# A two-block fp32 layer kernel: tile 0's chain to its first expert picks moved ahead of tile 1's last attention steps

## The reference

```python
cols_lat, cols_ctx = h_lat @ w_in, h_ctx @ w_in          # 256 latent, 256 context tokens
mla_lat = mla_mixer(...)      # 4 heads; latent queries, 512 keys; softmax(q k^T) v
ml_lat  = mlstm_mixer(...)    # 4 heads, two directions, gated linear attention, head norm
x  = x + gt1 * (concat([mla_lat, ml_lat]) @ w_out)
h2 = rmsnorm(x, g_norm2) * (1.0 + sc2) + sh2
x  = x + gt2 * peer(h2, ...)

def peer(xb):                                             # per tile of 128 tokens
    q = (xb @ w_pq).reshape(128, 8, 2, 128)
    s = einsum('thpd,hpkd->thpk', q, sub_keys)            # 8 heads x 2 x 128 keys
    sv, si = top_k(s, 16)                                 # then the 16 best of the 16 x 16 sums
    ...                                                   # -> eidx: 8 x 16 experts per token
    act = gelu(einsum('thkd,td->thk', expert_u[eidx], xb))
    return einsum('thk,thkd->td', g * act, expert_v[eidx])
```

## Time and profile before

| | |
|---|---|
| median of 3 runs | 1698.18 us (1697.4 to 1699.87) |
| profiled execution, first to last instruction | 1697.5 us; no other time of that execution is given |
| mean granted TensorE clock | 0.943 |
| TensorE matmul busy | 1465.2 us (86%) |
| VectorE busy | 1274.4 us (75%) |
| ScalarE busy | 554.8 us (33%) |
| GpSimd busy | 604.5 us (36%) |
| read from HBM | 436.23 MB, 258 GB/s over the span |

### The profile page before, as it was taken

How to read it: one execution, slowest core, us unless ns; L and a number is a source line. 1 busy time by engine, 2 the same in 40 slices (tenths; PEclk the granted TensorE clock), 3 DMA queues, 4 the chain that set the end, 5 groups by cost and what they waited for, 6 DMA issues and landing times.

```text
span 1697.5 us, 22640 instructions
## 1 busy us (share of the span) xinstructions
PE 1465.2 (86%) x7548; PEld 942.4 (56%) x7548; DVE 1274.4 (75%) x2708; ACT 554.8 (33%) x1549; POOL 604.5 (36%) x611
## 2 busy tenths in 40 slices
PE   7998999896969577646648999999999999999997
PEld 2645574343435122212213797699944797699953
DVE  1687777777777777778877687489986688479985
ACT  2234334443434243323322264222201254322210
POOL 0004036777777777777774002100011002100010
PEclk9999999998989799868768999999999999999999
DMA  9885059999999999999999541275553432085141
GB/s 365 304 289 219 24 218 405 409 409 409 409 403 407 409 403 409 390 398 405 398 405 384 193 147 51 77 259 174 175 181 105 149 116 85 28 296 161 51 156 67
DMA packets 170745, 438.77 MB, mean 258 GB/s; under 512 B 12531, under 2 KB 59027, under 8 KB 170500
## 3 DMA queue, kind: packets, MB, share of 16 engines
q0 software_dynamic: 81824, 299.86, 45.1%
q1 hardware_dynamic: 88806, 137.46, 23.3%
HBM read 436.23 MB, written 1.05 MB: 258 GB/s over the span
## 4 chain that ended last, share of the span: by engine, by line
PE 58%; DMA 12%; POOL 10%; DVE 9%; issue 6%; ACT 2%; DVEq 2%; SPq 1%; ACTq 0%; POOLq 0%
PE psum L908 19%; DMA arena<-in_expert_u,indices 11%; PE psum L1313 7%; POOL arena L1497 5%; POOL arena L1490 4%; PE psum L895 3%; PE psum L914 3%; PE psum L896 3%; PE psum L939 2%; DVE arena L2532 2%; PE psum L701 2%; PE psum L1279 2%; PE psum L584 2%; PE psum L1243 2%; PE psum L681 1%
## 5 line engine op out<-in xcount | busy, mean ns | idle before, releaser
L2532 DVE CUSTOM_DVE_ANT_0 arena<-arena,psum 128x1024 f32<-128x1024 f32 x256 | 312.6, 1221 | 142.5 <-DMA arena<-in_expert_u,indices 121.9
L895 PE MATMUL psum<-arena 128*128 128x512 f32 x380 | 237.9, 712 | 184.7 <-ACT arena L1809 182.9
L1490 POOL DMA_INDIRECT arena<-in_expert_u,indices x256 | 259.6, 1014 | 93.4 <-issue 66.3
L1497 POOL DMA_INDIRECT arena<-in_expert_v,indices x255 | 246.9, 968 | 82.6 <-issue 68.6
L895 PEld LDWEIGHTS psum<-arena 128*128 128x128 f32 x380 | 68.0, 213 | 310.0 <-ACT arena L1809 289.0
L896 PE MATMUL psum<-arena 128*128 128x512 f32 x380 | 221.4, 668 | 0.0
L1432 POOL TENSOR_TENSOR small<-small 128x1 f32<-128x1 f32 (+5 forms) x30 | 32.1, 1070 | 485.4 <-DVE small L2738 191.8
L908 PE MATMUL psum<-activations_T,weight_ring 128*128 128x128 f32 x1664 | 194.5, 275 | 0.0
L908 PEld LDWEIGHTS psum<-activations_T,weight_ring 128*128 128x128 f32 x1664 | 190.3, 192 | 1.0 <-issue 0.8
L1797 ACT ACTIVATE activations_T<-activations_T 128x1 f32<-128x1 f32 x256 | 51.9, 203 | 392.9 <-DVE activations_T L2532 392.7
L896 PEld LDWEIGHTS psum<-arena 128*128 128x128 f32 x380 | 82.0, 216 | 109.7 <-issue 109.7
(11 more groups left out here) (499 smaller groups left out, 2478.3 us busy)
## 6 DMA issues: line engine op xcount, KB each, us to landing
weight_ring<-in_ffn_w_in SPq DMA_DIRECT2D x44, 1024.0 KB, 7.7
weight_ring<-in_w_in SPq DMA_DIRECT2D x14, 2048.0 KB, 9.2
weight_ring<-in_w_ada SPq DMA_DIRECT2D x8, 2048.0 KB, 11.2
arena<-in_ffn_w_out POOLq DMA_DIRECT2D x14, 1024.0 KB, 7.0
weight_ring<-in_w_out SPq DMA_DIRECT2D x6, 2048.0 KB, 8.5
weight_ring<-in_w_ada SPq DMA_DIRECT2D x16, 512.0 KB, 9.9
weight_ring<-in_w_pq SPq DMA_DIRECT2D x4, 2048.0 KB, 12.8
weight_ring<-in_ffn_w_out POOLq DMA_DIRECT2D x8, 1024.0 KB, 5.3
```

The source lines that it names most:

```text
L895: mm(o0, DIAG[:, j % ND, :], v_row(n)[:, 0:512], start=m == 0, stop=last)
L1490: nc.gpsimd.indirect_dma_start(u_row(g), None, a["expert_u"], bass.IndirectOffsetOnAxis(ap=where, axis=0)).then_inc(sem(f"u_row{g % NU}"), 16)
L1497: nc.gpsimd.indirect_dma_start(v_row(g), None, a["expert_v"], bass.IndirectOffsetOnAxis(ap=where, axis=0)).then_inc(sem(f"v_row{g % NV}"), 16)
L2532: ttr(out=u_row(n), in0=u_row(n), in1=h2, scale=1.0, scalar=0.0, op0=ALU.mult, op1=ALU.add, accum_out=DOT[:, i, m:m + 1]).then_inc(sem("u_ ...
```

## The change

The first two batches stay, but there DVE takes a step's maximum ahead of the modulation sums (L2075) and copies the step's values after them. From the third batch on the order is new on PE, DVE and ACT. On PE the seventh step (u = 6) comes after tile 0's output product and not before it; the eighth to tenth (u = 7, 8, 9) come in one row after the first scores of both heads. The low half of tile 1's output product, which used to run while DVE searched, comes after them. On ACT batch 3's exponentials stand behind the copy of the first scores, and batch 2's turned weights and value products come after those. On DVE batch 3's product and combination come behind the whole search, with the last maximum ahead and the last three value copies behind. The first scores go to `SC00` in another tile, since `SC` lies where the values `VM` of the late steps still are. POOL gets two waits: g = 0 waits for the last step's scores, g = 2 also for the last step's values.

```diff
+        SC00 = v(3584, 4, NKEYS, of=XT)
 @block.tensor
+            score_products(*BATCHES[2])
+            outputs = [bank_d(), bank_d()]
+            output(outputs[0], 0, 0, 0, 4)
+            output(outputs[1], 0, 1, 0, 1)
+            gated(0, o)
+            output(outputs[1], 0, 1, 1, 4)
+            for b in range(2):
+                output(outputs[b], 0, b, 4, KT).then_inc(d_full, 1)
+            mla()
+            spread(BATCHES[3][1])
             h2_turned(0)
-            mla()
             first_queries(0)
-            mla()
-            heads_taken = c["d"]
-            first_scores(0)
             score_products(*BATCHES[3])
+            first_scores(0)
+            weights_turned(2)
+            value_products(2, BATCHES[2][1])
+            first_queries(1)
+            first_scores(1)
+            for _ in range(3):
+                mla()
+            at["mla_last"] = heads_taken = c["d"]
             outputs = [bank_d() for b in range(2)]
+            h2_back(0, bank_d, sem("h2_back"))
             pe.wait_ge(d_free, heads_taken)
             output(outputs[0], 1, 0, 0, 4)
             output(outputs[1], 1, 1, 0, 4).then_inc(sem("wout_low"), 1)
-            value_products(2, BATCHES[2][1])
-            first_queries(1)
-            first_scores(1)
-            h2_back(0, bank_d, sem("h2_back"))
             weights_turned(3)
             value_products(3, BATCHES[3][1])
 @block.gpsimd
+                if g == 0:
+                    pool.wait_ge(a_full, at["mla_s"][7])
                 if g == 2:
                     pool.wait_ge(sem("ml_p"), 2 * len(BATCHES))
+                    pool.wait_ge(d_full, at["mla_last"])
 @block.scalar
+            exponentials(2)
+            gated(0)
...
+            mla()
             h2_turned(0)
-            mla()
-            exponentials(3)
-            mla()
             first_queries(0)
             first_scores(0)
+            exponentials(3)
+            weights_turned()
             heads_mixed(*BATCHES[2])
             first_queries(1)
             first_scores(1)
+            mla()
             pick_exp(0)
+            mla()
 @block.vector
+            for n in range(2):
+                mla_probabilities()
+                decayed_maxima(n)
+                mla()
+                mla_probabilities()
+                mixed(n)
+                combined()
+                mla_maximum()
+                modulation(10 + n, 11 + n)
...
+                mla_taken()
...
+            mla()
+            h2_end(0)
+            mla_probabilities()
+            decayed_maxima(3)
+            all_of(search(0))
+            mla_maximum()
+            mixed(3)
+            mla_probabilities()
+            dve.wait_ge(a_full, at["comb", 2])
+            combined()
+            for _ in range(3):
+                mla_taken()
```

More of the change, by code:

```diff
@@ L784, in _ @@
             spread(0)
-            for n, (i, hp) in enumerate(BATCHES[:3]):
+            for n, (i, hp) in enumerate(BATCHES[:2]):
                 mla()
                 score_products(i, hp)
[L788 to L793, removed]
-                    mla()
[L795 to L806, removed]
-                    mla()
+                modulation_sum(10 + n)
+                if n == 1:
+                    pe.wait_ge(sem("pool_sum"), 1)
+                    o = bank_d()
+                    mm(o, ONE, MACP, start=True, stop=True).then_inc(d_full, 1)
+                mla()
@@ L808, in _ @@
                 weights_turned(n)
                 spread(BATCHES[n + 1][1])
-                if n < 2:
-                    value_products(n, hp)
+                value_products(n, hp)
+            score_products(*BATCHES[2])
+            wout += [weights()[:, 0:4 * D].rearrange("p (k n) -> p k n", k=4) for half in range(2)]
+            outputs = [bank_d(), bank_d()]
+            output(outputs[0], 0, 0, 0, 4)
+            output(outputs[1], 0, 1, 0, 1)
+            o = bank_a()
+            at["gated"] = c["a"]
@@ L1705, in first_scores @@
                 o = full()
-                act.copy(SC[:, 0, 2 * hh:2 * hh + 2, :], o[:, 0:2 * P].rearrange("p (c k) -> p c k", c=2)).then_inc(a_free, 1)
+                act.copy(SC00[:, 2 * hh:2 * hh + 2, :], o[:, 0:2 * P].rearrange("p (c k) -> p c k", c=2)).then_inc(a_free, 1)
             def pick_exp(k):
@@ L1728, in weights_turned @@
                     act.copy(MLPT[:, hh, :, :], o.rearrange("p (s q) -> p s q", s=4)).then_inc(a_free, 1)
-            for n, (i, hp) in enumerate(BATCHES[:3]):
+            for n, (i, hp) in enumerate(BATCHES[:2]):
                 exponentials(n)
                 mla()
[L1733 to L1739, removed]
                 mla()
                 weights_turned()
-                if n < 2:
-                    heads_mixed(i, hp)
+                heads_mixed(i, hp)
+            exponentials(2)
+            gated(0)
+            for h in range(2):
+                act.wait_ge(sem("x_ready" if h else "x_half"), 1)
+                e = slice(h * 512, h * 512 + 512)
+                ins = af(XSQ[0][:, e], X[:, 0, e], ACT.Square, accum_out=SS[:, 16 + h:17 + h])
+            ins.then_inc(sem("ss_ready"), 1)
+            mla()
             h2_turned(0)
-            mla()
-            exponentials(3)
-            mla()
             first_queries(0)
             first_scores(0)
+            exponentials(3)
+            weights_turned()
             heads_mixed(*BATCHES[2])
@@ L2471, in _ @@
-                if n < 3:
-                    mla()
+                mla_taken()
+            dve.drain()
+            decayed_maxima(2)
+            mla_probabilities()
+            mean_of([(0, 4, VD)])
+            gate(0)
+            mixed(2)
+            combined()
+            dve.wait_ge(sem("g2_in"), 16)
+            stt(MODB[:, 2, :], MODB[:, 2, :], 1.0, G2[:, :], ALU.add, ALU.mult)
+            dve.drain()
+            for b in range(2):
+                e = slice(b * 512, (b + 1) * 512)
+                o = full()
+                tt(MTMP[:, b, :], o, MODB[:, 0, e], ALU.mult).then_inc(d_free, 1)
+                dve.drain()
+                tt(X[:, 0, e], X[:, 0, e], MTMP[:, b, :], ALU.add).then_inc(sem("x_ready" if b else "x_half"), 1)
+                dve.drain()
+                tt(H2[0][:, e], X[:, 0, e], MODB[:, 2, e], ALU.mult)
```

55 lines of the change are left out of this document (21 added, 34 removed).

## The result

The changed kernel takes 1706.67 us (median of 5 runs, 1705.10 to 1708.22) against 1698.18 us for the kernel before: ratio 1.0047, 95% interval 1.0036 to 1.0057. It is 8.5 us slower; 7.8 were forecast. The profiled execution spans 1706.2 us (8.7 more than before) at a mean granted clock of 0.938 (0.943 before); its time, 1708.22 us, is the highest of the five. The totals say little: VectorE's group of dot products has the same busy time, and idles 1.3 us more than in the earlier trace rows.

The account below looks back on a forecast made before the run. DMA engines were taken to bound the picks, the end moving with when gathers run without a stop. Queue loss 7.2 less backlog 1.3 is 5.9, plus clock 1.9 is 7.8: 1698.18 to 1706.0 us, range 1700.5 to 1710 (own range 1702.6 to 1709).

Parts of the forecast that it names:

- First part: Up to the first scores: VectorE's new order and later MLA steps bring them at 215.9, 5.7 us earlier.
- Rival D: Gated heads come later than 193.8 by a us or more, delaying first scores: 1707 to 1708; chance 0.05.
- Second part: From first scores to TensorE's sums: work becomes a chain with two waits, V gather 8 at 268.2, 7.2 us later.
- would show it: List of expected profile signs, such as first gather at 229 to 231, pick 2 near 238, V gather 8 near 268 to 270.
- Clock: TensorE's half clock behind the two new waits: 1.9 us taken, from 0 to 3.8.
- 0 for the second: Clock price of TensorE's second wait taken as 0, since its followers wait for VectorE anyway up to the low outputs.
- Rival C: Both waits drop TensorE's clock for longer, low outputs at half speed: +9.7, 1707.9, up to 1710; chance 0.2.
- I take 1.3: Smaller DMA backlog at V gather 8, by 0.55 MB, gives back 1.3 us of the 7.2; ends 0 and 1.3.
- the 1.5 of the joints: Uncertainty of +-1.5 us for some twelve chain joints read from rows with neighbours of another kind.
- Small edits: `SC00` copy, POOL's wait for the last values, w_pq's later third slice and the earlier `keys` load: 0 each.
- A: Faster: DMA traffic bounds and its first gather starts 3.5 us earlier, so 1694.7; chance 0.07.
- B: No change: exponentials in other work's shadow, TensorE's waits about one us each, about 1699.5; chance 0.15.

Follow-up runs that it names:

- short fill: Changed kernel with 12 idle 128x128 matmuls on TensorE in each of the two 3.1 us waits: 1703.91 us, ratio 1.0033.
- pick 3 early: Changed kernel with tile 1's two low output products moved behind batch 3's turned weights and value products on TensorE: 1705.37 us, ratio 1.0041.
- without the load: Changed kernel with w_pq's third slice not loaded but for a corner, gathers as many: 1707.14 us, ratio 1.0058.
- early VectorE edit: Kernel before; in batches 0 and 1 VectorE takes the next MLA maximum ahead of the modulation sums, the values' copy behind: 1696.75 us, ratio 0.9988.
- both waits shorter: Changed kernel; ScalarE copies batch 2's turned weights before batch 3's exponentials, VectorE takes last probabilities before batch 3's mixing, value copies before its combination: 1700.89 us.

## Why the prediction was right

The forecast of 1706.0 us is 0.7 off the median and inside its range, and most of its steps stand: the loss was made where it said, by the waits and the order that it named. Two terms were mis-sized, and in part it was lucky.

**First part.** Value products of batch 1 at 186.4 (measured 186.39), output product 189.35 (189.33), MLA step 203.6 (203.60), turned h2 208.8 (208.79), first scores 215.9 (215.84). The steps are right; that the dates agree to a tenth is luck, since the other profiles with this order have the first scores anywhere from 213.53 to 215.59. Counted from the 24 small matmuls ahead of the change, they come after 72.34 to 73.43 us in the seven profiles with the new order and after 78.18 to 78.72 in the four with the old one, 5.3 us sooner on average, where 5.7 were forecast. Rival D is out.

**Second part.** With its 1.9 for the first clock drop added to each date from the value products on, the chain said pick 0 231.9 (232.18), h2 turned back 240.0 (239.80), low outputs 240.9 (241.44), pick 3 248.9 (249.62), last value products 249.7 (250.07), sums 267.8 (268.30), V gather 8 270.1 (270.52). The waits were forecast at 3.4 and 3.2 us and are 3.09 and 3.08. What "would show it" said of the first gather (229 to 231) left that 1.9 out and missed by 1.2.

**Clock.** The step "0 for the second" was wrong in its reason: the second drop came, at 0.50 for a whole stretch, and the followers up to the low outputs are on the chain. It cost 1.2, the first 1.6, together 2.85 by the short fill; the text had 1.9, with 3.8 as the upper end. That the first drop came in the profiled execution was luck: it came in one of the three profiles that leave this wait as it was, and no run tells how often the timed executions had it. Rival C was right for this execution that both waits drop the clock, not in the size, and not in low outputs at half speed (7.03 us; 7.13 in the earlier trace rows). By the rule that it took from the Trainium skill ("TensorE: Matmul & The Clock Gate", section "HAM oscillation — how this bites in real kernels") a long idle gap puts the array at half clock each time. The changed kernel's trace agrees at both waits (0.66 and 0.50), and the runs with pick 3 early and without the load do not: the same 3.09 us were followed by full clock there.

**Backlog.** The step "I take 1.3" was mis-sized. Bytes left at V gather 8 were to differ by 0.55 MB and differ by 0.27 (2.12 and 1.85), and from V gather 8 to the reciprocal root 0.47 us was paid back, of which nothing up to the last gather. The rows between 1.7 and 2.4 MB scatter by more, so it is not told from nothing. Its reason, that DMA and not POOL is the bound and a smaller backlog is therefore worth its full time, holds from 2.1 to 4.3 MB and not below. Both terms err to the same side: at V gather 8 the sum had 9.1 and it was 9.54 (0.9 of clock too little, 0.5 of it taken back by joints that were shorter), and the backlog had 1.3 and it was 0.47. Against that, 0.37 us came back behind the root, which no run explains. 9.54 - 0.47 - 0.37 = 8.7 of span, where the sum had 7.8.

**Range and offset.** The lower end of the forecast's own range takes off the 1.5 of the joints, the upper end does not add it. That "the median of runs stands 0.7 above the span" sets one execution's span against the median of others: an execution's time is about 2.0 above its own span (1708.22 and 1706.2). It does no harm, as the 7.8 are added to the median.

**Small edits.** POOL's new wait for the last values was to be met at 237, ahead of the combination. It was not: L654, the values themselves, released pick 2 at 240.78. The forecast was 237.8, or 239.7 with the first clock drop; the rest is the values at half clock. No run takes this wait alone; as V gather 8 ended last, and stayed where it was when pick 3 went at once, it should have cost nothing. The late load of `w_pq` at 0 was right for this kernel, as the run without it shows; in the kernel before the same delay cost 6.9 us. The text's reason (covered by the picks) was not the right one: the load fell into the idle time that pick 3's wait had opened.

**Rivals.** A is out: the first gather did come 1.3 us earlier and was worth nothing. B is out as the kernel stands, but it named the way: with ScalarE's exponentials in a shadow and TensorE's waits at 0.73 and 1.71 us, it is 1700.89, where B said about 1699.5.

## What to carry to other kernels

When work is moved behind a point to reach that point sooner, count from the point to the next place where the engine is the bound: TensorE did the same work here, 5 to 6 us were won at the first scores, and 10.7 us of the profiled execution went into two waits that the old order had filled with work, and into the half clock behind them. Then look at the order on the engines that serve those waits; moving two neighbours on ScalarE and VectorE brought 5.8 us of it back. And a stage fed by DMA has two limits, the date of the last permit and the bytes still queued at it: before costing a delay, see which of them it stands on. Near their meeting point, as in the kernel before, a delay of either kind cost most of its length, and an earlier permit alone won nothing.

## What the runs showed of the hardware

- A wait of 3.09 us ahead of the same instruction was followed by a granted clock of 0.66 in one execution and of 1.00 in two others (220 to 225 us; value products 3.48, 2.05 and 2.05 us). In the early VectorE edit the clock was 0.66 over 237 to 242 us behind two waits of only 0.77 and 0.68 us. So the length of the last wait alone does not tell whether the clock falls. The waits of 0.41 and 0.40 us in the short fill and of 0.73 and 1.71 us with both waits shorter were followed by full clock.
- A float32 matmul of 128x128 shows as two instructions, 0.115 us each: 24 calls took 5.52 us (x48).
